# A ring of 18 panel slots, expert products in one run, a split first gather, and an earlier router in a two-block kernel

## The chip, the cores and the metric

The kernel runs on one core of one Trainium2 chip. The metric is the device time of one execution in microseconds (us); less is better.

## What is computed

The input is 512 tokens of width 1024 in fp32. A first block (token mixer, cross-attention, MLP) is followed by a second one. The part at the end of the second block is what most of the change touches:

```python
# second block, in outline
x = x + mixer(...)                        # windowed attention (8 heads) and gated linear attention, then w_out
logits = rmsnorm(x) @ w_router            # 16 experts
# every expert takes the 64 tokens of the largest affinity
# for its tokens: y = (silu(t @ w_gate) * (t @ w_up)) @ w_down, scaled by the affinity, added into x
x = x + sigmoid(rmsnorm(x) @ w_ple_gate) * (p @ w_ple)
out = rmsnorm(x)
```

Each expert has three matrices of 1024x1024 in fp32 (4 MB each). The 16 experts together read 201 MB, which is most of the 328 MB that the kernel reads.

## The kernel before

The program is written by hand for each engine: a block for TensorE (PE), ScalarE (ACT), VectorE (DVE), GpSimd (POOL) and SyncE (SP), with semaphores between them. No planner orders anything; the order in each block is the order on the engine. SP issues nearly all loads, in one queue. PSUM has 8 banks. `STAGES` (line 47) lists each use of a bank in program order; `bank_claim` waits until the last user of a bank has released it, `bank_written` until it is full, and `bank_done` until it is read out.

**Dense products** (`product_steps`, line 574, matmul at L609). Weights come in parts of 512 KB into four raw buffers (`raw`, L247; the load is L2740). POOL splits each part into a high and a low fp32r half (`split_parts_of`, L648 and L649). Each product of 128x128 by 512 is three matmuls on the halves. In `attn_pe` (L1492) and `gla_pe` such steps fill the time between dependent steps.

**Attention** (`attn_pe`, `attn_act` L1525, `attn_dve` L1566). For a pair of heads: scores (L1500), mask (DVE, L1578), maxima (L1585, L1586), powers (ACT, L1544 to L1546), shares (DVE, L1591 to L1594), turns (L1506), outputs (L1515). Between these, ACT reads the banks of the projections that fill TensorE's time (`att_evacuate`, L1480). For the first pair it reads three banks and then computes the powers of heads 0 and 1.

**Router** (PE L2188 to L2246). When the product out2 is done, its rows are turned (`norm_ffn`), a p product (`ple_product`, L1991) follows, then the router (L2211), its sum over four groups (L2217), the softmax on DVE and ACT, the turn affT (L2225), eight rounds of top-8 on DVE (L2658, L2659), and the slots. Seven further p products and `keep_busy` fillers (L501) stand between. ACT copies each p product out (L1997), stores them to HBM in `p_keep` and scales the rows (L424).

**Experts** (L1819 to L1985 and `expert_pe`, L1907). Experts go in 8 pairs; the two of a pair use the two halves of the array's columns (`x_rows`). For a pair: gather its tokens (L1895, 32 matmuls for each half of the features), DVE applies a gain (L1962), then the products gate, up and down (`expert_product`, L1850, matmul at L1864), the turn of the hidden values (L1920) and the scatter (L1882). A product reads 8 panels of 1 MB in four quarters of two panels. In each pair the order on TensorE is gate, scatter of the pair before, up, first half of the next gather, turn, second half, down. DVE adds the scattered rows to X (`add_dve`, L716) ahead of the hidden product (L1977). For pair 0 both halves of the gather stand ahead of everything.

**The ring.** The 192 panels go through 16 slots (`ring`, L1431), loaded by SP in order (`expert_load`, L1842). Slots are parts of memory that earlier stages use. So SP waits ahead of panel 0 for the last ygla bank, ahead of 6 for the last out2 bank, of 12 for the router and of 14 for the last p product. From panel 16 on it waits for the quarter that used the slot last: `x_used` counts quarters; at the fourth of each product it rises behind a `drain`. Behind the panels SP loads `p_keep` back (L2762) and the parts of w_ple_gate (L2764), for the last product.

## Time and profile before

| | before |
|---|---|
| median of 3 runs | 1996.89 us (1995.45 to 1999.15) |
| profiled execution, its own time | 1992.46 us |
| its span | 1990.7 us |
| PE busy | 1902.8 us, 96% |
| DVE, ACT, POOL busy | 781.1, 553.4, 998.0 us |
| HBM read | 328.01 MB |
| DMA in the slices of 1443 to 1940 us | 421 GB/s in nearly all |

Times in the rows are microseconds from the start of the span. The profiled execution is one execution; its own time lies 4.4 us below the median of the runs. A busy PE need not be at its peak. `PEclk` is the granted clock as a share of full speed.

### The profile page before, as it was taken

How to read it: one execution, taken by the hardware profiler on the slowest of the kernel's cores; microseconds unless marked ns; L12 is line 12 of the kernel's file. 1: busy time of each engine (PE TensorE's matmuls, PEld its weight loads, DVE VectorE, ACT ScalarE, POOL GpSimd, SP SyncE). 2: the span in 40 equal slices, each digit the busy share in tenths (PEclk: the TensorE clock that was granted, in tenths of full speed). 3: DMA queues.
4: the chain of work that ended last, by engine and by line, in shares of the span. 5: the costliest groups of instructions: out<-in, count | busy, mean ns of one | idle time of the engine just before them, and what ended most of it. 6: DMA issues, size and time to landing. Idle time of an engine off the chain costs nothing.

```text
span 1990.7 us, 23274 instructions
## 1 busy us (share of the span) xinstructions
PE 1902.8 (96%) x9434; PEld 1390.7 (70%) x9434; DVE 781.1 (39%) x1187; ACT 553.4 (28%) x1120; POOL 998.0 (50%) x568
## 2 busy tenths in 40 slices
PE   7999998999999999999989999999999999999988
PEld 6878887678788888888767768887854444434436
DVE  2455668561413301323545375554241221212124
ACT  4534438342412200211123442332230000000025
POOL 5796766657368877887555587446600000000012
PEclk9999999999999999999999999999999999999999
DMA  5321113322123223323322222212689999999982
GB/s 184 94 74 41 35 53 116 117 70 100 54 74 95 95 95 96 96 99 97 113 64 64 64 74 85 61 57 81 260 343 421 421 421 421 420 422 421 421 351 74
DMA packets 92697, 335.81 MB, mean 169 GB/s; under 512 B 7696, under 2 KB 9488, under 8 KB 67760
## 3 DMA queue, kind: packets, MB, share of 16 engines
q1 hardware_dynamic: 88864, 321.29, 43.2%
q10 hardware_dynamic: 3584, 12.52, 1.7%
q8 instruction: 75, 1.23, 0.3%
q0 software_dynamic: 144, 0.52, 0.1%
q14 instruction: 30, 0.25, 0.0%
HBM read 328.01 MB, written 6.29 MB: 168 GB/s over the span
## 4 chain that ended last, share of the span: by engine, by line
PE 78%; DMA 7%; POOL 6%; DVE 4%; ACT 3%; issue 1%; SPq 1%; PEldq 0%; ACTq 0%; DVEq 0%; PEld 0%; POOLq 0%
PE bank L609 48%; PE bank L1864 12%; DMA arena<-in_w_exp_up 3%; PE bank L1895 3%; POOL shared_r L667 2%; DMA shared<-in_w_exp_up 1%; DMA arena<-in_w_exp_gate 1%; DMA arena<-in_w_exp_down 1%; PE bank L786 1%; PE bank L630 1%; POOL shared_r L648 1%; POOL shared_r L649 1%; PE bank L1882 1%; PE bank L1068 1%; PE bank L1450 1%
## 5 line engine op out<-in xcount | busy, mean ns | idle before, releaser
L609 PE MATMUL bank<-shared_r 128*128 128x512 f32 (+1 forms) x3888 | 898.7, 387 | 18.0 <-POOL shared_r L667 7.3
L609 PEld LDWEIGHTS bank<-shared_r 128*128 128x128 f32 x3888 | 703.2, 189 | 174.4 <-issue 14.7
L648 POOL TENSOR_TENSOR shared_r<-shared,small 128x1024 fp32r<-128x1024 f32 (+1 forms) x172 | 335.3, 1949 | 847.9 <-DMA shared<-in_w_ple_gate 493.7
L649 POOL TENSOR_TENSOR shared_r<-shared,shared_r 128x1024 fp32r<-128x1024 f32 (+1 forms) x172 | 424.3, 2467 | 13.5
L1864 PE MATMUL bank<-arena 128*64 128x512 f32 x768 | 170.5, 595 | 9.8 <-DMA arena<-in_w_exp_up 3.8
L1864 PE MATMUL bank<-shared,arena 128*64 128x512 f32 x768 | 170.8, 594 | 9.4 <-DMA shared<-in_w_exp_gate 3.2
L609 PE MATMUL bank<-shared_r,arena_r 128*128 128x512 f32 x768 | 176.1, 391 | 0.0
L609 PEld LDWEIGHTS bank<-shared_r,arena_r 128*128 128x128 f32 x768 | 144.2, 188 | 31.6
L667 POOL TENSOR_TENSOR shared_r<-shared,shared_r 128x1024 fp32r<-128x1024 f32 x40 | 102.0, 2550 | 91.8 <-ACT shared_r L658 91.8
L1864 PEld LDWEIGHTS bank<-shared,arena 128*64 128x64 f32 x768 | 57.4, 137 | 116.9 <-issue 106.7
L1864 PEld LDWEIGHTS bank<-arena 128*64 128x64 f32 x768 | 56.0, 137 | 117.3 <-issue 103.3
L2344 ACT ACTIVATE arena<-arena 128x512 f32<-128x512 f32 x32 | 20.2, 633 | 219.3 <-DVE arena L2554 218.9
L609 PE MATMUL bank<-arena_r,shared_r 128*128 128x512 f32 x336 | 79.2, 396 | 0.8 <-issue 0.8
L609 PEld LDWEIGHTS bank<-arena_r,shared_r 128*128 128x128 f32 x336 | 62.9, 188 | 16.3 <-issue 1.2
L716 DVE TENSOR_TENSOR X<-bank,X 128x512 f32<-128x512 f32 x56 | 34.1, 680 | 97.0 <-PE bank L1882 97.0
L786 PE MATMUL bank<-arena 128*128 128x64 f32 x448 | 57.0, 271 | 11.7 <-DVE arena L924 6.6
L495 DVE SCALAR_TENSOR_TENSOR X<-bank,small,X 128x512 f32<-128x512 f32 x16 | 11.9, 746 | 142.4 <-PE bank L609 142.4
L786 PEld LDWEIGHTS bank<-arena 128*128 128x128 f32 x448 | 55.0, 191 | 17.2 <-issue 10.6
L2554 DVE TENSOR_SCALAR arena<-bank 128x512 f32<-128x512 f32 x32 | 21.9, 684 | 106.9 <-PE bank L609 106.5
L1895 PEld LDWEIGHTS bank<-arena 128*128 128x128 f32 x512 | 58.3, 192 | 7.8 <-issue 7.8
L1895 PE MATMUL bank<-arena 128*128 128x128 f32 x512 | 60.1, 276 | 1.9 <-issue 1.9
L1977 DVE TENSOR_TENSOR bc<-bank,bc 128x512 f32<-128x512 f32 x16 | 16.7, 1043 | 114.2 <-PE bank L1864 112.4
(428 smaller groups left out, 2072.4 us busy)
## 6 DMA issues: line engine op xcount, KB each, us to landing
shared<-in_w_in SPq DMA_DIRECT2D x80, 512.0 KB, 3.6
arena<-in_w_exp_gate SPq DMA_DIRECT2D x32, 1024.0 KB, 25.5
shared<-in_w_exp_gate SPq DMA_DIRECT2D x32, 1024.0 KB, 25.8
shared<-in_w_exp_up SPq DMA_DIRECT2D x32, 1024.0 KB, 23.4
arena<-in_w_exp_up SPq DMA_DIRECT2D x32, 1024.0 KB, 24.2
arena<-in_w_exp_down SPq DMA_DIRECT2D x32, 1024.0 KB, 25.7
shared<-in_w_exp_down SPq DMA_DIRECT2D x32, 1024.0 KB, 26.1
shared<-in_w_up SPq DMA_DIRECT2D x32, 512.0 KB, 3.6
```

Of the source, the lines that this page charges most:

```text
L609: ins = pe.matmul(dst, W_, x_, start=first, stop=final)
L630: ins = pe.matmul(bank[:, :], x[b][:, k, j * P:(j + 1) * P], halves[a][:, kk, :], start=k == 0 and (a, b) == (0, 0), stop=k == KT - 1 and ...
L648: link(pool.tensor_tensor(hi, raw(p), small[:, 18:19].to_broadcast([P, hi.shape[1]]), ALU.add))
L649: pool.tensor_tensor(lo, raw(p), hi.bitcast(F32), ALU.subtract).then_inc(S_("w_split"), 1)
L667: pool.tensor_tensor(lo, raw(p), hi.bitcast(F32), ALU.subtract).then_inc(S_("w_split"), 1)
L716: bank_release(dve.tensor_tensor(xs, bank[:, :], xs, ALU.add), n)
L786: ins = pe.matmul(bank[:, h * 64:(h + 1) * 64], HKL[g % 4][:, h, :], HQL[g % 4][:, h, :], start=True, stop=True)
L1068: ins = pe.matmul(bank[:, d * 256:d * 256 + CW], WT[:, d, s, t * P:(t + 1) * P], VM[:, s, h, :], start=(s == srcs[0]), stop=(s == srcs[-1]))
L1864: ins = pe.matmul(banks_[h][x_rows(e), :], stay, panel[:, kk, h * 512:(h + 1) * 512], start=k == 0, stop=k == KT - 1)
L1895: ins = pe.matmul(bank[:, dd * P:(dd + 1) * P], XS[:, j, d * P:(d + 1) * P], OH[:, j].rearrange("p e c -> p (e c)"), start=j == 0, stop=j ...
L2344: link(act.activation(HR[:, f % 4, :], HR[:, f % 4, :], ACT.Square))
L2554: bank_release(dve.tensor_scalar(HR[:, f % 4, :], bank[:, :], 0.0, None, ALU.max), n)
```

## The change

- The ring has 18 slots; the two new ones (`spare`) come first. SP waits for ygla ahead of panel 2, for the last split of out2 ahead of 8, for the last out2 bank ahead of 10, for the router ahead of 14 and for the last p product ahead of 16.
- The wait for a free slot is for `x_used`, which counts three quarters of each product, or for the written bank at the fourth; the `drain` is gone.
- On TensorE gate and up follow each other; the scatter of the pair before comes behind them. On DVE the additions come behind the hidden products.
- For pair 0: half 0 of the gather, two quarters of gate, half 1, the other two quarters.
- The router stands ahead of all p products; one filler instead of three stands ahead of slotT.
- In the attention the powers of head 0 stand ahead of the first evacuations.
- The load of norm_final moves from POOL to SP. The loads of w_ple_gate stand ahead of that of `p_keep`, both in other places of memory.

The diff, cut to its core (the squares of the last norm and the scratch of POOL's descriptors, which also change place or size, are left out, as are the like moves in the order of ACT's copies and DVE's reads):

```diff
-RING = 16
+RING = 18
-ARENA = 26960
+ARENA = 26768
...
+    spare_at = -(-nc.sbuf_base // 32) * 32
+    spare = sb("spare", [P, 2 * XPANEL])
+    spare_r = nc.alloc_sbuf_tensor_at("spare_r", [P, 2 * XPANEL], F32R, offset=spare_at)
...
     def raw(p):
-        return shared[:, 2 * PANEL + 1024 * (p % 4):2 * PANEL + 1024 * (p % 4) + parts[p]["kp"] * parts[p]["n"]]
+        of, at, n = shared, 2 * PANEL + 1024 * (p % 4), parts[p]["kp"] * parts[p]["n"]
+        if p >= late:
+            of, at = arena, ring_at + 6 * XPANEL + 1024 * (p % 4)
+        return of[:, at:at + n]
...
-        if p >= late + 2 and (p - late) % 6 >= 2:
-            at = ring_at + XPANEL * (4 + (p - late) % 6 - 2)
+        if p >= late and (p - late) % 6 < 2:
+            at = XPANEL * ((p - late) % 6)
+            return spare_r[:, at:at + n], spare_r[:, at + n:at + 2 * n]
+        if p >= late:
+            at = ring_at + XPANEL * ((p - late) % 6)
             return arena_r[:, at:at + n], arena_r[:, at + n:at + 2 * n]
...
+    spares = [spare[:, i * XPANEL:(i + 1) * XPANEL] for i in range(2)]
-    ring = inner[0:6] + outer[4:8] + outer[2:4] + outer[0:2] + inner[6:8]
+    ring = spares + inner[0:6] + outer[4:8] + outer[2:4] + outer[0:2] + inner[6:8]
...
         for p in range(NH // 2 + 1):
...
-            else:
-                att_evacuate(act, done, place["score", 1, 3] + 1)
             if p < NH // 2:
                 powers(2 * p)
-                if p:
-                    att_evacuate(act, done, place["out", p - 1, 0] + 1)
+                att_evacuate(act, done, place["out", p - 1, 0] + 1 if p else place["score", 1, 3] + 1)
                 powers(2 * p + 1)
...
-    x_order = [("x", 0, 0), ("x", 0, 1), ("o", 0, 0)]
+    x_order = [("x", 0, 0), ("o", 0, 0)]
     for i in range(PAIRS):
-        x_order += [("g", i, h) for h in range(2)]
+        x_order += [("g", i, h) for h in range(2)] + ([("x", 0, 1)] if i == 0 else []) + [("u", i, h) for h in range(2)]
         if i:
             x_order += [("s", i - 1, r) for r in range(8)]
-        x_order += [("u", i, h) for h in range(2)]
...
+    def panels_used(eng, q):
+        c, w, i = q // 2 % 4, q // 8 % 3, q // 24
+        if c < 3:
+            eng.wait_ge(S_("x_used"), 3 * (q // 8) + c + 1)
+        else:
+            bank_written(eng, x_bank["guy"[w], i, 1])
+
+    def slots_over(eng, slot):
+        q = slot + (2 * 4 * 3 * PAIRS - 1 - slot) // RING * RING
+        panels_used(eng, q)
...
     def expert_load(sp, q):
...
         if q >= RING:
-            sp.wait_ge(S_("x_used"), (q - RING) // 2 + 1)
+            panels_used(sp, q - RING)
...
-    def expert_product(pe, name, w, i):
-        banks_ = [bank_claim(pe, x_bank[name, i, h]) for h in range(2)]
-        for c in range(4):
+    def expert_product(pe, name, w, i, quarters=range(4)):
+        banks_ = [bank_claim(pe, x_bank[name, i, h]) if 0 in quarters else banks[BANK[x_bank[name, i, h]]] for h in range(2)]
+        for c in quarters:
...
             else:
-                ins.then_inc(bank_full[BANK[x_bank[name, i, 1]]], 1)
-                pe.drain().then_inc(S_("x_used"), 1)
+                bank_ready(ins, x_bank[name, i, 1])
...
     def expert_gather(pe, i, half):
...
-        if half == 0:
-            return
+        if half == (i > 0):
+            expert_weights(pe, i)
+
+    def expert_weights(pe, i):
         n = x_bank["o", i, 0]
...
     def expert_pe(pe, i):
-        expert_product(pe, "g", 0, i)
+        if i == 0:
+            expert_gather(pe, 0, 0)
+            expert_product(pe, "g", 0, 0, range(0, 2))
+            expert_gather(pe, 0, 1)
+            expert_product(pe, "g", 0, 0, range(2, 4))
+        else:
+            expert_product(pe, "g", 0, i)
+        expert_product(pe, "u", 1, i)
         if i:
             bank_done(pe, x_bank["o", i - 1, 0])
             expert_scatter(pe, i - 1)
-        expert_product(pe, "u", 1, i)
...
     def expert_dve(dve, i):
         expert_choice(dve, i + 1)
-        if i:
-            add_dve(dve, [x_bank["s", i - 1, r] for r in range(8)])
         for h in range(2):
...
+        if i:
+            add_dve(dve, [x_bank["s", i - 1, r] for r in range(8)])
         expert_gathered(dve, i + 1)
...
-        bank_written(pool, cell_out(H - 1, ST - 1))
-        pool.dma_start(bc[:, 0:D], A["norm_final"].partition_broadcast(P)).then_inc(S_("nf_in"), 16)
...
         router_turn(pe, out2, 1)
-        for k in range(2):
-            bank_done(pe, BASE["turn_p"] + k)
-        pe.wait_ge(S_("wp_in"), 16)
-        ple_product(pe, 0)
         pe.wait_ge(S_("wr_in"), 16)
         n = BASE["router"]
...
         bank_ready(ins, n)
+        for k in range(2):
+            bank_done(pe, BASE["turn_p"] + k)
+        pe.wait_ge(S_("wp_in"), 16)
         bank_done(pe, n)
...
-        ple_product(pe, 1)
+        ple_product(pe, 0)
         keep_busy(pe, BASE["affT"], 2, 128)
...
-        for g in range(2, 8):
+        for g in range(1, 8):
             ple_product(pe, g)
-        keep_busy(pe, BASE["slotT"], 3)
+        keep_busy(pe, BASE["slotT"], 1)
...
-        for half_ in range(2):
-            expert_gather(pe, 0, half_)
...
         for p in range(4, late):
+            if p == panels[PB["xout"]]["parts"][0]:
+                bank_written(sp, cell_out(H - 1, ST - 1))
+                sp.dma_start(bc[:, 0:D], A["norm_final"].partition_broadcast(P)).then_inc(S_("nf_in"), 16)
             load(p)
-        bank_done(sp, BASE["ygla"] + 7)
         for q in range(2 * 4 * 3 * PAIRS):
-            if q == 6:
+            if q == 2:
+                bank_done(sp, BASE["ygla"] + 7)
+            if q == 8:
+                sp.wait_ge(S_("w_split"), parts[late - 1]["split"])
+            if q == 10:
                 bank_written(sp, out2[7])
-            if q == 12:
+            if q == 14:
                 bank_done(sp, BASE["router"])
-            if q == 14:
+            if q == 16:
                 bank_written(sp, ple[7])
             expert_load(sp, q)
-        sp.wait_ge(S_("x_used"), (2 * 4 * 3 * PAIRS - RING + 2) // 2)
-        sp.dma_start(PP[:, :, :, :], p_keep.rearrange("p (i j d) -> p i j d", i=2, j=ST)).then_inc(S_("pp_in"), 16)
-        sp.wait_ge(S_("x_used"), (2 * 4 * 3 * PAIRS - RING + 10) // 2)
+        slots_over(sp, 0)
+        slots_over(sp, 16)
         for p in range(late, late + 4):
             load(p)
+        slots_over(sp, 2)
+        sp.dma_start(PP[:, :, :, :], p_keep.rearrange("p (i j d) -> p i j d", i=2, j=ST)).then_inc(S_("pp_in"), 16)
```

## Rows read from the trace of the kernel before

**Rows 1.** Windows; columns: stretch, length, busy time by engine, PEclk, DMA share, GB/s.
```profile
1600.00:1700.00 100.00, 98.45 (x525) 47.00 (x524) 23.59 (x35) 7.07 (x10) 0.00 (x0) 1.00 1.01 421
```

**Rows 2.** The chain that ended last, 1450 to 1600 us; columns: start, length, what.
```profile
1453.78 10.30 PE bank L1991 x24
...
1469.84 7.15 PE bank L1895 x64
...
1477.43 13.88 PE bank L1864 x64
...
1514.49 13.88 PE bank L1864 x64
...
1569.68 13.88 PE bank L1864 x64
```

**Rows 3.** Timeline of TensorE, the last pair; start, length, line, operation, idle before and releaser.
```profile
1888.00 3.91 PE L1882 MATMUL bank<-arena_r 128*128 128x512 f32 x16 [0.27 <-issue]
...
1905.10 3.65 PE L1864 MATMUL bank<-shared,arena 128*64 128x512 f32 x16 [1.31 <-DMA shared<-in_w_exp_up]
1910.28 1.09 PE L1920 MATMUL bank<-ident,bc 128*128 128x128 f32 x8 [1.52 <-DVE bc L1977]
...
1924.98 3.65 PE L1864 MATMUL bank<-arena 128*64 128x512 f32 x16 [1.22 <-DMA arena<-in_w_exp_down]
```

**Rows 4.** Timeline of all engines, 1395 to 1482 us: issues of SP, and POOL's last split.
```profile
1413.51 3.14 SPq L1848 DMA_DIRECT2D arena<-in_w_exp_gate  x6
...
1435.12 2.39 POOL L649 TENSOR_TENSOR shared_r<-shared,shared_r 128x1024 fp32r<-128x1024 f32 x1
...
1443.92 0.80 SPq L1848 DMA_DIRECT2D shared<-in_w_exp_gate  x2
...
1464.11 0.80 SPq L1848 DMA_DIRECT2D arena<-in_w_exp_up  x2
...
1481.05 7.67 SPq L1848 DMA_DIRECT2D arena<-in_w_exp_down  x6
```

**Rows 5.** Windows around the holes in the stream.
```profile
1432.50:1444.50 12.00, 12.00 (x59) 10.00 (x58) 2.65 (x4) 2.17 (x6) 4.29 (x2) 1.00 0.02 7
...
1464.00:1477.00 13.00, 13.00 (x95) 10.78 (x94) 4.85 (x11) 0.60 (x1) 0.00 (x0) 1.00 0.98 358
1477.00:1482.50 5.50, 5.50 (x28) 1.97 (x28) 3.17 (x5) 0.00 (x0) 0.00 (x0) 1.00 0.16 34
```

**Rows 6.** Timeline of all engines, the start of the attention.
```profile
1022.47 0.23 DVE L1586 TENSOR_SCALAR small<-small 128x4 f32<-128x4 f32 x1
...
1027.16 1.28 ACT L1544 ACT_TABLE_LOAD   x1
1027.72 4.37 PE L609 MATMUL bank<-shared_r 128*128 128x512 f32 x18
...
1030.87 0.28 ACT L1546 ACTIVATE small<-small 128x4 f32<-128x4 f32 x1
...
1031.49 2.36 POOL L649 TENSOR_TENSOR shared_r<-shared,shared_r 128x1024 fp32r<-128x1024 f32 x1
...
1031.68 3.37 DVE L1594 TENSOR_SCALAR arena<-arena,small 128x384 f32<-128x384 f32 x4
...
1037.16 2.40 PE L1506 MATMUL bank<-ident,arena 128*128 128x128 f32 x10 [5.08 <-DVE arena L1578]
...
1039.21 6.28 PE L609 MATMUL bank<-shared_r 128*128 128x512 f32 x18
```

**Rows 7.** Window behind the gap in the attention.
```profile
1038.00:1040.00 2.00, 2.00 (x10) 1.90 (x9) 0.37 (x1) 1.43 (x3) 0.00 (x0) 0.50 0.00 0
```

**Rows 8.** Timeline, DVE's half of the last norm_ffn turns.
```profile
1445.45 1.41 DVE L435 TENSOR_SCALAR shared<-bank,PT 128x512 f32<-128x512 f32 x2 [0.84 <-PE bank L445]
```

**Rows 9.** Timeline of POOL, the load of norm_final.
```profile
461.71 0.70 POOL L2062 DMA_DIRECT2D bc<-in_norm_final  x1
```

**Rows 10.** TensorE's waits: releaser, us in total, times, longest.
```profile
PE bank L1807 <- DVE arena L1795: 2.6, 1, 2.6
```

More of the change, by code:

```diff
@@ L1962, in expert_gathered, with expert_weighted @@
             bank_release(dve.tensor_tensor(XG[:, 4 * half:4 * half + 4, :], bank[:, :].rearrange("p (d c) -> p d c", d=4), gain, ALU.mult), n)
+            if half == (i > 0):
+                expert_weighted(dve, i)
+    def expert_weighted(dve, i):
         n = x_bank["o", i, 0]
@@ L2390, in _ @@
         router_act(act, out2)
-        ple_evacuate(act, 0)
         act.wait_ge(S_("rmax"), 1)
         act.activation(AFF[:, :, :], AFF[:, :, :], ACT.Exp).then_inc(S_("rexp"), 1)
-        ple_evacuate(act, 1)
+        ple_evacuate(act, 0)
         for j in range(ST):
             scale_rows(act, j)
-            ple_evacuate(act, 2 + j)
-        for g in range(2 + ST, 8):
+            ple_evacuate(act, 1 + j)
+        for g in range(1 + ST, 8):
             ple_evacuate(act, g)
@@ L2795 @@
     from concourse.bass_utils import run_bass_kernel_spmd as _run
-    nc = _bacc.Bacc("TRN2", target_bir_lowering=False, num_devices=1)
+    nc = _bacc.Bacc("TRN2", target_bir_lowering=False, num_devices=1, dynamic_dma_scratch_size=1024)
     arrays, args = {}, {}
```

2 lines of the change are left out of this document (1 added, 1 removed).

## The prediction, made before the changed kernel ran

> **What bounds the kernel now.** I read the windows of the expert stage first. From about 1482 us to 1925 us the DMA engines are full: a stretch of 100 us shows a share of 1.01 and 421 GB/s [rows 1]. The stage streams 192 panels of 1.049 MB, so one panel costs 2.49 us and a pair of panels (one quarter of a product) 4.98 us. A pair of experts has 24 panels, 59.8 us. TensorE needs less: two down products one pair of experts apart start at 1514.49 and 1569.68, 55.2 us [rows 2]. On its own it would have ended the last down product at 1514.5 + 7 x 55.2 + 13.9 - 7.8 (no gather in the last pair) = 1906.9; it ends at 1928.6, since the last quarter waits for its panels and starts at 1924.98 [rows 3]. From there to the end of the span (1990.7) 65.7 us follow, with the last scatter and the ple_gate product, and no wait for a transfer. The end is therefore the landing of the last panel plus this tail. What counts is how long the DMA engines stood idle before 1482 while panels were still to come.
>
> The timeline shows why they did. Six panels go from 1413.51, the next only at 1443.92 when the last out2 bank is written, the last two of the 16 slots at 1464.11 behind the last p product, and the seventeenth panel at 1481.05, when the first quarter has freed a slot [rows 4]. The windows show the holes: 7 GB/s from 1432.5 to 1444.5, and 34 GB/s from 1477 to 1482.5 [rows 5].
>
> Second, the attention. TensorE has a gap of 5.1 us from 1032.1 to 1037.16. The timeline leads through VectorE to ScalarE, which started the powers of head 0 only at 1027.16, behind three evacuations, though their input was there at 1022.70 [rows 6]. Behind the gap the granted clock is 0.50, the lower level (1.2 GHz) [rows 7].
>
> **The ring, and the order of loads.** Ahead of the wait for out2 stand panels 0 to 7 now, and 8 and 9 wait only for the last split of out2, which POOL ends at 1437.5 [rows 4]. Six panels were through at 1432.5; two more (5.0 us) last to 1437.5, and 8 and 9 fill 1439 to 1444. Panels 10 to 13 go at 1443.9, 14 and 15 behind the router; all are through at about 1459.5. Then the engines idle until 16 and 17 come, which wait for the last p product. So most of the first hole moves to 1460; but by the time of the first quarter 18 panels are in instead of 16. This is worth 2 x 2.49 = 5.0 us, no more, since the ring was full before and is full now.
>
> **Router ahead of p product 0.** The router claims the bank that the eighth norm_ffn turn leaves, and VectorE ends that at 1446.86 [rows 8]. It took 1.92 us from 1447.28; from 1446.95 it ends at 1448.87: 0.3 us sooner, not the 1.9 us of the p product ahead of it. Everything to the gather comes 0.3 us sooner. Seven p products now follow affT instead of six, 1.72 us each (10.30 us for six) [rows 2]: the last ends at 1465.5 instead of 1464.1. Picks come at 1466.1, so one filler is enough and nothing idles. Panels 16 and 17 go at 1465.5 instead of 1464.1; with the 2 MB that ScalarE stores they took 12.9 us to about 1477 [rows 5], so now to 1478.5 or 1479.
>
> **Gather split.** Both halves of the gather (7.15 us) stood ahead of the gate product, which began at 1477.43 [rows 2]. Now half 0 runs from 1469.5 to 1473.1; VectorE's 0.7 us for its gain, hidden before, lie open; the product starts at 1473.85. The first quarter (3.5 us) frees its slots at 1477.45, 3.6 us sooner; the second at 1480.9; half 1 and another 0.7 us follow; the third ends at 1488.7, the fourth at 1492.1. The stream: panels 18 and 19 from 1478.9, 20 and 21 to 1488.9, 22 issued at 1488.7 and moving at 1490.1, a hole of 1.2 us. Before, panel 16 began to move at 1482.55, so that at 1490.1 the stream stood at 19.05. Now it stands at 22, ahead by 2.95 panels: **7.3 us**, ring and split together. TensorE is 1 us later at the end of that gate product; of its 22 us of slack that costs nothing.
>
> **Products in one run, scatter behind them.** Drains that go (0.3 us each) give nothing while panels are the limit. Two points had to be worked out. (a) The last pair: the last up quarter can start 19.9 us before the last panel lands. It takes 3.65, the scatter 3.9, turn and evacuation 1.5, three down quarters 10.7 [rows 3]: 19.8 us. TensorE arrives as the last panel does: 0 us, with no margin, where the scatter's 3.9 us were margin before. (b) VectorE has eight additions of 0.7 us behind the hidden products; TensorE claims the banks in that order and slower. 0 us. norm_final moves from POOL's queue, where its issue took 0.70 us [rows 9], to SP's: POOL waits for TensorE behind it, and SP loads four parts ahead of use. 0 us; without that cover 0.7 us either way. The ple_gate and p_keep loads stand behind the last panel in SP's queue, and the tail didn't wait for them: 0 us.
>
> **First powers ahead of banks.** ScalarE starts at 1022.75. From table load to the sums of head 0 took 4.0 us (1027.16 to 1031.15), so VectorE gets head 0 at 1026.75. Three evacuations (1.8 us) and head 1 (2.6 us) follow: 1031.15. TensorE claims the first evacuated bank at 1029.2, and it is free at 1027.4: no new wait. Now VectorE's shares of head 1 stand where those of head 0 stood. Its four multiplications took 3.37 us there, with POOL's L649 active from 1031.49 to 1033.85; undisturbed they take 1.41 [rows 6]. I take it that head 1 meets the same: VectorE is through at 1035.05 instead of 1036.78, and TensorE goes on at 1035.45 instead of 1037.16: **1.7 us**, leaving a gap of 3.4 us. Undisturbed it would be 3.7 us; nothing and 3.7 are the bounds. The Trainium skill, SBUF — State Buffer, section "SBUF: two separate sides", says that VectorE and GpSimd lock a pair of ports for a whole instruction, and that whichever starts first gets it. By that rule VectorE may as well win here, and the sum would be 2.0 us more.
>
> The clock: 18 matmuls of the same product took 6.28 us behind the gap and 4.37 us ahead of it; of the ten transposes' 2.40 us half is the clock's: 3.1 us [rows 6, 7]. The next longest gap inside the kernel is one of 2.6 us, and the clock stayed up behind it [rows 10]. 3.4 us lie between; nearer to 2.6, so I take it that it stays up: **3.0 us**. From 1037 on TensorE has no gap up to 1151, and what POOL splits behind that is released by TensorE, so both gains reach the end.
>
> **Sum** against the profiled execution: 7.3 + 1.7 + 3.0 = 12.0 us, span 1990.7 to 1978.7, its time 1992.5 to 1980.5. The median of the three runs is 4.4 us above the profiled time: 1996.9 - 12.0 = **1984.9**. A measurement tells about 0.2% (4 us) from no change.
>
> **Rivals.**
> 1. The clock still falls behind the gap of 3.4 us. Gain 9.0, **1987.9**. For it: a gap of 5.1 us does it. Against: 2.6 doesn't. 0.24.
> 2. VectorE gets ahead of POOL: gap 1.4 us, gain 14.0, **1982.9**. Against it: POOL was ahead by 0.2 us. 0.10.
> 3. The last pair is late, or the hole at 1489 wider: at the last down quarter each microsecond is one at the end. Late by 2 us, with a hole of 4.2 us: gain 7, **1990**. 0.12.
> 4. The ring brings no lead, because 16 and 17 are not in before the first quarter asks for more. Then 2.3 us of the 7.3 and little of the attention are left: gain 3, **1994**. 0.05.
> 5. Slower: the stretch between up and down products, in which no slot comes free, grows by the scatter from 8.7 to 12.6 us in pairs 1 to 6, and the queue runs dry in each. It decides when less than some 16 us of loads (3.3 pairs of panels) are in flight at the end of the up product. By the rates above 4.6 are in flight in pair 1, and more later, so I don't expect it. If it were so: 3.9 us in each of six pairs, 23 us, less 12: **2008**. 0.04.
>
> The forecast keeps 0.45. **Range** 1979.5 to 1993: forecast and rivals 1 to 3, with the bounds of each and 2 us for the medians. Faster 0.91 (all but rivals 4 and 5), same 0.05, slower 0.04.
>
> **What would show it.** Windows: a hole near 1460 to 1466, hardly one between 1477 and 1489, 421 GB/s from there to the last panel (all less what the attention gains). Last down quarter at about 1913. TensorE's wait at L1506 3.4 us, and a granted clock of 1.00 behind it. I am wrong if the last quarter isn't released by a transfer, if GB/s falls between up and down products in the middle pairs, or if the clock shows 0.50 behind the gap.

## The result, and the profile after

The changed kernel's median is 1988.25 us over 5 executions (1985.09 to 1992.09), beside 1995.45 us (1992.79 to 1999.15, 5 executions) for the kernel before on the same chip. The ratio is 0.9961, with a 95% interval of 0.9948 to 0.9974: about 7.8 us less, between 5.2 and 10.4 (the two medians differ by 7.2). The forecast was a gain of 12.0 us and a time of 1984.9, with a range of 1979.5 to 1993.0.

| | before | after |
|---|---|---|
| profiled execution, its own time | 1992.46 us | 1989.56 us |
| its span | 1990.7 us | 1987.8 us |
| its mean granted clock | 0.996 | 0.991 |
| PE, DVE, ACT, POOL busy | 1902.8, 781.1, 553.4, 998.0 | 1905.6, 782.7, 553.5, 997.0 us |
| HBM read | 328.01 MB | 328.01 MB |

The two spans differ by 2.9 us only, since the two executions had different luck with the clock ahead of the changed places (experiment 4). So I compare stretches that begin at an event of the same work: in the attention from the scores of heads 2 and 3, first half, to their second half; in the expert stage from the issue of the first panel (1413.51 before, 1416.68 after).

**The attention.** Timeline of all engines of the changed kernel, 1018 to 1048 us (L618 is L609 of before, L1516 is L1506, L1601 is L1594, L1554 and L1556 are L1544 and L1546):

```profile
1018.25 1.28 ACT L1554 ACT_TABLE_LOAD   x1
...
1027.34 0.62 ACT L1554 ACTIVATE arena<-arena,small 128x384 f32<-128x384 f32 x1 [7.80 <-DVE small L1593]
...
1029.76 0.28 ACT L1556 ACTIVATE small<-small 128x4 f32<-128x4 f32 x1
...
1031.05 1.35 PE L1510 MATMUL bank<-arena 64*128 64x256 f32 x8
...
1031.82 1.41 DVE L1601 TENSOR_SCALAR arena<-arena,small 128x384 f32<-128x384 f32 x4
...
1034.41 1.89 POOL L657 TENSOR_TENSOR shared_r<-shared,small 128x1024 fp32r<-128x1024 f32 x1 [2.86 <-PE bank L618]
...
1034.78 4.83 DVE L1601 TENSOR_SCALAR arena<-arena,small 128x384 f32<-128x384 f32 x4
1036.39 2.35 POOL L658 TENSOR_TENSOR shared_r<-shared,shared_r 128x1024 fp32r<-128x1024 f32 x1
...
1039.99 2.22 PE L1516 MATMUL bank<-ident,arena 128*128 128x128 f32 x10 [3.29 <-DVE arena L1585]
...
1041.86 5.18 PE L618 MATMUL bank<-shared_r 128*128 128x512 f32 x18
...
1046.97 1.35 PE L1510 MATMUL bank<-arena 64*128 64x384 f32 x8
```

ScalarE now starts with the powers of head 0, and VectorE's shares of head 0 take 1.41 us instead of 3.37 [rows 6]. ScalarE's table load stands at 1018.25 now, in time in which ScalarE has nothing else to do; before, it stood at 1027.16 and delayed head 0 [rows 6]. The shares of head 1 take 4.83 us, with both steps of POOL's split beside them. TensorE's gap is 3.29 us instead of 5.08. Behind it the same ten transposes and 18 matmuls take 2.22 and 5.18 us (2.40 and 6.28 before; 4.37 for 18 at the full clock [rows 6]): the clock still falls. From scores to scores it is 15.92 us instead of 18.98.

**The start of the stream.** Timeline of SP, 1395 to 1500 us (L1867 is L1848 of before):

```profile
1416.68 0.94 SPq L1867 DMA_DIRECT2D spare<-in_w_exp_gate  x2
1417.67 3.69 SPq L1867 DMA_DIRECT2D arena<-in_w_exp_gate  x6
1440.70 12.93 SPq L1867 DMA_DIRECT2D shared<-in_w_exp_up  x8
1468.84 0.80 SPq L1867 DMA_DIRECT2D arena<-in_w_exp_down  x2
1481.10 1.01 SPq L1867 DMA_DIRECT2D spare<-in_w_exp_down  x2
1484.53 9.84 SPq L1867 DMA_DIRECT2D arena<-in_w_exp_down  x4
1496.18 0.89 SPq L1867 DMA_DIRECT2D arena<-in_w_exp_gate  x2
```

Timeline of TensorE, 1465 to 1500 us (gather L1913, expert products L1883):

```profile
1472.69 3.74 PE L1913 MATMUL bank<-arena 128*128 128x128 f32 x32
...
1477.41 3.65 PE L1883 MATMUL bank<-spare,arena 128*64 128x512 f32 x16 [0.55 <-DVE arena L1988]
1480.87 3.63 PE L1883 MATMUL bank<-arena 128*64 128x512 f32 x16
1484.43 3.84 PE L1913 MATMUL bank<-arena 128*128 128x128 f32 x32
1489.05 7.09 PE L1883 MATMUL bank<-arena 128*64 128x512 f32 x32 [0.78 <-DVE arena L1988]
```

Windows (stretch, length, busy time by engine, PEclk, DMA share, GB/s) in the same profile:

```profile
1464.00:1470.00 6.00, 6.00 (x19) 2.58 (x17) 5.20 (x12) 4.17 (x7) 0.00 (x0) 1.00 0.12 27
1480.00:1484.00 4.00, 4.00 (x22) 1.54 (x18) 0.00 (x0) 0.00 (x0) 0.00 (x0) 1.00 0.81 283
1481.50:1482.00 0.50, 0.50 (x4) 0.17 (x2) 0.00 (x0) 0.00 (x0) 0.00 (x0) 1.00 0.11 41
1484.00:1492.00 8.00, 7.22 (x50) 4.71 (x48) 1.98 (x3) 0.00 (x0) 0.00 (x0) 1.00 1.01 428
1492.00:1500.00 8.00, 8.00 (x40) 2.73 (x38) 0.00 (x0) 3.42 (x3) 0.00 (x0) 1.00 0.82 286
1493.00:1493.50 0.50, 0.50 (x6) 0.21 (x4) 0.00 (x0) 0.00 (x0) 0.00 (x0) 1.00 0.00 0
1540.00:1640.00 100.00, 100.00 (x536) 48.04 (x534) 22.20 (x33) 8.69 (x12) 0.00 (x0) 1.00 1.01 421
```

The hole is at 1464 to 1470, as forecast. Behind it the stream is nearly whole, but not quite: at a mean of 283 and 286 instead of 421 GB/s it loses 1.3 us from 1480 to 1484 and 2.6 us from 1492 to 1500. These are short stops and not a slower stream throughout: within them it stands at 41 GB/s from 1481.5 to 1482 and at 0 from 1493 to 1493.5, just behind the issue of the next pair of panels. From 1500 to 1900 it runs at 421 or 422 GB/s.

**The end of the stream.** Timeline of TensorE, 1895 to 1930 us (scatter L1900, turn L1946):

```profile
1901.72 3.65 PE L1883 MATMUL bank<-arena 128*64 128x512 f32 x16 [1.31 <-DMA arena<-in_w_exp_up]
1905.31 3.92 PE L1900 MATMUL bank<-arena_r 128*128 128x512 f32 x16
1909.07 1.03 PE L1946 MATMUL bank<-ident,bc 128*128 128x128 f32 x8
1910.56 7.09 PE L1883 MATMUL bank<-arena 128*64 128x512 f32 x32 [0.45 <-ACT arena L1961]
1917.45 3.63 PE L1883 MATMUL bank<-shared,arena 128*64 128x512 f32 x16
1922.05 3.65 PE L1883 MATMUL bank<-shared,arena 128*64 128x512 f32 x16 [0.97 <-DMA shared<-in_w_exp_down]
```

The last down quarter still waits for its panels. It starts 505.37 us behind the first panel's issue, where it was 1924.98 - 1413.51 = 511.47. The tail behind it is 65.75 us, as before (65.7).

### The profile page after: what moved, and what is told of

Same layout as the page of the kernel before. It is cut to its first block, busy times and chain, and to the rows that moved or that the text cites. A ratio compares the mean times of both kernels' runs of the same rounds, so it can differ in the third digit from the quotient of the medians.

```text
span 1987.8 us, 23241 instructions
## 1 busy us (share of the span) xinstructions
PE 1905.6 (96%) x9430; PEld 1395.6 (70%) x9430; DVE 782.7 (39%) x1187; ACT 553.5 (28%) x1120; POOL 997.0 (50%) x567
## 3 DMA queue, kind: packets, MB, share of 16 engines
HBM read 328.01 MB, written 6.29 MB: 168 GB/s over the span
## 4 chain that ended last, share of the span: by engine, by line
PE 78%; DMA 7%; POOL 7%; DVE 4%; ACT 3%; issue 1%; SPq 0%; ACTq 0%; DVEq 0%; POOLq 0%
PE bank L618 48%; PE bank L1883 11%; PE bank L1913 3%; DMA arena<-in_w_exp_up 3%; DMA shared<-in_w_exp_up 3%; POOL shared_r L676 2%; PE bank L1900 1%; DMA shared<-in_w_exp_down 1%; PE bank L795 1%; POOL shared_r L658 1%; PE bank L639 1%; POOL shared_r L657 1%; PE bank L1077 1%; PE bank L1460 1%; PE bank L2022 1%
## 5 line engine op out<-in xcount | busy, mean ns | idle before, releaser
L618 PE MATMUL bank<-shared_r 128*128 128x512 f32 (+1 forms) x3840 | 891.1, 388 | 15.0 <-POOL shared_r L676 6.7
L618 PEld LDWEIGHTS bank<-shared_r 128*128 128x128 f32 x3840 | 697.9, 190 | 169.4 <-issue 14.7
L658 POOL TENSOR_TENSOR shared_r<-shared,shared_r 128x1024 fp32r<-128x1024 f32 (+1 forms) x170 | 419.5, 2468 | 13.4
L657 POOL TENSOR_TENSOR spare_r<-arena,small 128x1024 fp32r<-128x1024 f32 x2 | 3.8, 1895 | 482.8 <-DMA arena<-in_w_ple_gate 482.8
L618 PE MATMUL bank<-shared_r,arena_r 128*128 128x512 f32 x768 | 176.1, 391 | 0.0
L618 PEld LDWEIGHTS bank<-shared_r,arena_r 128*128 128x128 f32 x768 | 144.2, 188 | 31.5
L1883 PE MATMUL bank<-arena 128*64 128x512 f32 x688 | 154.6, 599 | 11.0 <-DMA arena<-in_w_exp_up 9.8
L1883 PE MATMUL bank<-shared,arena 128*64 128x512 f32 x672 | 147.7, 593 | 8.6 <-DMA shared<-in_w_exp_up 7.7
L676 POOL TENSOR_TENSOR shared_r<-shared,shared_r 128x1024 fp32r<-128x1024 f32 x38 | 96.8, 2547 | 96.0 <-ACT shared_r L667 96.0
L1883 PEld LDWEIGHTS bank<-arena 128*64 128x64 f32 x688 | 49.6, 138 | 108.9 <-issue 93.5
L1883 PEld LDWEIGHTS bank<-shared,arena 128*64 128x64 f32 x672 | 48.3, 137 | 105.1 <-issue 93.9
L2370 ACT ACTIVATE arena<-arena 128x512 f32<-128x512 f32 x32 | 20.3, 633 | 219.2 <-DVE arena L2579 218.7
L618 PE MATMUL bank<-arena_r,shared_r 128*128 128x512 f32 x336 | 79.5, 396 | 0.8 <-issue 0.8
L618 PEld LDWEIGHTS bank<-arena_r,shared_r 128*128 128x128 f32 x336 | 63.1, 188 | 16.4 <-issue 1.2
L1913 PEld LDWEIGHTS bank<-arena 128*128 128x128 f32 x512 | 58.9, 192 | 2.1 <-issue 1.6
L1913 PE MATMUL bank<-arena 128*128 128x128 f32 x512 | 60.0, 275 | 0.0
```

What stands on the lines that cost most here:

```text
L618: ins = pe.matmul(dst, W_, x_, start=first, stop=final)
L657: link(pool.tensor_tensor(hi, raw(p), small[:, 18:19].to_broadcast([P, hi.shape[1]]), ALU.add))
L658: pool.tensor_tensor(lo, raw(p), hi.bitcast(F32), ALU.subtract).then_inc(S_("w_split"), 1)
L676: pool.tensor_tensor(lo, raw(p), hi.bitcast(F32), ALU.subtract).then_inc(S_("w_split"), 1)
L1883: ins = pe.matmul(banks_[h][x_rows(e), :], stay, panel[:, kk, h * 512:(h + 1) * 512], start=k == 0, stop=k == KT - 1)
L1913: ins = pe.matmul(bank[:, dd * P:(dd + 1) * P], XS[:, j, d * P:(d + 1) * P], OH[:, j].rearrange("p e c -> p (e c)"), start=j == 0, stop=j ...
```

## The experiments

"Stream to up" and "stream to down" are the times from the first panel's issue to the last up and the last down quarter; "attention" is the stretch from scores to scores; all from the one profile of each kernel. The time is the median of all executions, the ratio is to the kernel before on the same chip.

| kernel | time us | ratio (95%) | attention | stream to up | stream to down |
|---|---|---|---|---|---|
| before | 1995.45 | 1 | 18.98 | 491.59 | 511.47 |
| after | 1988.25 | 0.9961 (0.9948 to 0.9974) | 15.92 | 485.04 | 505.37 |
| e1_attention_only | 1995.65 | 0.9988 (0.9979 to 0.9997) | 15.96 | 491.87 | 511.75 |
| e2_all_but_attention | 1990.94 | 0.9971 (0.9959 to 0.9982) | 18.90 | 485.09 | 505.10 |
| e3_gather_not_split | 1989.93 | 0.9961 (0.9948 to 0.9975) | 15.94 | 486.33 | 507.3 |
| e4_ring_of_16 | 1992.63 | 0.9980 (0.9971 to 0.9989) | 15.93 | 490.17 | 510.40 |
| e5_fill_two_gaps | 1987.05 | 0.9952 (0.9939 to 0.9965) | 14.31 | 485.85 | 505.73 |
| e6_scatter_between | 1987.97 | 0.9956 (0.9943 to 0.9968) | 15.90 | 484.90 | 504.92 |
| e7_router_behind_p | 1989.6 | 0.9960 (0.9946 to 0.9974) | 15.92 | 485.12 | 505.03 |
| e8_before_filled | 1993.95 | 0.9988 (0.9979 to 0.9997) | 16.10 | 491.52 | 511.40 |
| e9_fill_five_gaps | 1985.81 | 0.9941 (0.9928 to 0.9955) | 14.32 | 483.93 | 503.88 |
| e9_again | 1985.06 | 0.9940 (0.9929 to 0.9952) | 14.31 | 484.30 | 504.26 |
| e10_fill_the_right_gaps | 1989.55 | 0.9961 (0.9947 to 0.9974) | 14.31 | 484.05 | 505.10 |

The kernel before had medians of 1997.44 (beside e1 to e4), 1996.88 (e5, e6, e8, e9) and 1997.64 (e7, e9_again, e10).

### 1. The attention alone, and all the rest

e1 is the kernel before with the new order of the powers; e2 is the changed kernel with the old order:

```diff
-            else:
-                att_evacuate(act, done, place["score", 1, 3] + 1)
             if p < NH // 2:
                 powers(2 * p)
-                if p:
-                    att_evacuate(act, done, place["out", p - 1, 0] + 1)
+                att_evacuate(act, done, place["out", p - 1, 0] + 1 if p else place["score", 1, 3] + 1)
```

Expected of e1: 

> The kernel before with the attention edit alone (powers of head 0 ahead of the three evacuations). Theory A (mine): TensorE's gap at the first turns shrinks from 5.1 to about 3.3 us, 1.8 us gained for good; the clock still falls there for about half as long, 3.4 instead of 6.8 us, so 1.3 us more in the mean: 3.1 us below the kernel before at the same clock elsewhere. The expert stage is as before: holes of 12 us and 5.5 us in the stream. Theory B (the lower mean clock in the changed kernel comes from the attention edit): the granted clock over the run is lower than that of the kernel before by 0.003 or more here too, and the gain is 0 or less.

Expected of e2: 

> The changed kernel with the attention as before. Theory A: TensorE's gap is 5.1 us again, with a low clock of 6.8 us behind it; the expert stage keeps its lead of 6.1 us from the first expert load to the last panel, so the time is 6 us below the kernel before, 3 us above the changed kernel at the same clock elsewhere. Theory B (the new places in memory or the moved load of norm_final lower the clock in the first 1000 us): the clock over the run is lower than that of the kernel before in all runs, and the start of the attention is reached 3 us or more later than in the kernel before.

Measured: 0.9988 and 0.9971, that is 2.4 and 5.8 us of 1997, each to about 2 us, together 8.2 where the whole change has 7.8. So the two halves add up within these intervals, and nothing shows that one eats the other's gain. By stretches e1 gains 3.0 us in the attention and nothing in the stream, e2 0.1 and 6.4 us. The gap in e1 is 3.34 us, with a granted clock behind it as in the changed kernel. Theory A holds for both; theory B of e1 does not (its mean clock over the executions is 0.9928, that of the kernel before 0.9919).

### 2. The parts of the lead

e3 has both halves of the first gather ahead of the gate product, e4 the ring of 16 slots with SP's waits at the panels two lower, e7 the router behind p product 0 (and with it the order of ACT's copies and the three fillers of before); cut to the core:

```diff
e3:
             expert_gather(pe, 0, 0)
-            expert_product(pe, "g", 0, 0, range(0, 2))
             expert_gather(pe, 0, 1)
-            expert_product(pe, "g", 0, 0, range(2, 4))
+            expert_product(pe, "g", 0, 0)
...
e4:
-RING = 18
+RING = 16
...
-    ring = spares + inner[0:6] + outer[4:8] + outer[2:4] + outer[0:2] + inner[6:8]
+    ring = inner[0:6] + outer[4:8] + outer[2:4] + outer[0:2] + inner[6:8]
...
e7:
+        for k in range(2):
+            bank_done(pe, BASE["turn_p"] + k)
+        pe.wait_ge(S_("wp_in"), 16)
+        ple_product(pe, 0)
         pe.wait_ge(S_("wr_in"), 16)
         n = BASE["router"]
...
```

Expected of e3: 

> The changed kernel with both halves of the first gather ahead of the gate product. Theory A: the first quarter ends 3 us later, and the DMA engines stand idle until then, but the small holes of 1480 to 1500 (3.7 us of transfer lost there in the changed kernel) close: lead over the kernel before 4.5 to 5 us instead of 6.1, so the split is worth 1 to 1.5 us, not the 2 us of the forecast. Rival: the small holes are of the ring's order of loads and stay; then the lead falls to 3 us or less, and the split is worth 3 us.

Expected of e4: 

> The changed kernel with 16 slots (without the two new ones), all other parts of the change in place. Theory A: two panels less are in before the first quarter, so the last panel lands 5.0 us later than in the changed kernel, counted from the first expert load: lead over the kernel before 1 us. Rival (the lead comes from the earlier first quarter, and the ring's two slots only fill a hole that would be filled anyway): the lead stays above 3 us.

Expected of e7: 

> The changed kernel with the router behind p product 0, as before. Theory (the router's move brings 0.3 us to the first gather, since the norm_ffn turns set its start): the router's first matmul 1.9 us later behind the last turn's end than in the changed kernel less what it waited there (1.33 us idle), so the first gather 0.2 to 0.6 us later, the last up quarter 0.2 to 0.6 us later behind the first expert load; time 1988 to 1990, not to be told from 1988.3. Rival (the move is worth its whole p product): the gather and the last up quarter 1.9 us later, 1990 to 1991.

The lead is how much sooner behind the first panel's issue a quarter starts than in the kernels with the old order. Three kernels have the old ring, gather and router (before, e1, e8), eight have all that is new (after, e2, e5, e6, e7 but for the router, e9 twice, e10). At the last up quarter the former stand at 491.52 to 491.87, mean 491.66, the latter at 483.93 to 485.85, mean 484.79: 6.9 us of lead. At the last down quarter it is 511.54 less 504.92: **6.6 us**, with single profiles up to about 1 us to either side. e4 lacks 5.4 us of the lead at the last up quarter, so the two slots bring 5.4; e3 lacks 1.5, so the split brings 1.5, each with that same scatter. The rival of e4 is refuted.

Of e3 theory A is right, in its size and in its reason. Windows of e3, and of the changed kernel for the second stretch:

```profile
1480.00:1484.00 4.00, 4.00 (x20) 1.29 (x18) 0.57 (x1) 0.00 (x0) 0.00 (x0) 1.00 0.25 51
1484.00:1500.00 16.00, 16.00 (x78) 5.35 (x76) 0.00 (x0) 3.42 (x3) 0.00 (x0) 1.00 1.01 422
```

```profile
1484.00:1500.00 16.00, 15.22 (x88) 7.44 (x86) 1.98 (x3) 3.42 (x3) 0.00 (x0) 1.00 0.92 357
```

Without the split there is one long hole, until the first quarter has freed its slots, and none behind it. It is so in all four kernels without the split: in 16 us that begin 5 us behind the issue that the first quarter released, before, e1, e3 and e8 have 424 or 425 GB/s, and the nine with the split 351 to 379. e4 is among the nine, with 353, so it isn't the ring. The split frees the first slots sooner and gives part of that back: in the changed kernel SP issues no panel from 1484.90 to 1492.75, while TensorE does half 1 of the gather and the third quarter, and the stream stops at 1493.

In the times e4 shows its loss, just clear of the intervals (0.9980 beside 0.9961); e3 does not.

e7 is the router's move by itself. Its first gather comes 1473.64 - 1417.43 = 56.21 us behind the first panel's issue, 56.01 in the changed kernel: 0.2 us, not 1.9. The last up quarter is the same to 0.1 us.

e3's last pair shows how thin the cover there is. Timeline of its TensorE, 1895 to 1930 us:

```profile
1901.06 5.35 PE L1883 MATMUL bank<-arena 128*64 128x512 f32 x16 [2.36 <-DMA arena<-in_w_exp_up]
1906.34 3.92 PE L1900 MATMUL bank<-arena_r 128*128 128x512 f32 x16
...
1918.53 7.06 PE L1883 MATMUL bank<-shared,arena 128*64 128x512 f32 x32
```

Here TensorE waited 2.36 us for an up panel, the granted clock fell (0.63 in the window 1902.6 to 1906), and the quarter took 5.35 us instead of 3.65. The last two down quarters then run on without a wait: the end was set by TensorE, 0.9 us behind where the panels would have set it (507.3, against 504.9 of the others and the 1.5 us that this kernel is behind them). In the other profiles the last quarter waits for its panels.

### 3. The scatter's place

e6 has the scatter, and VectorE's additions, between gate and up again, without the drains and with the ring of 18 (cut to TensorE's part):

```diff
-        expert_product(pe, "u", 1, i)
         if i:
             bank_done(pe, x_bank["o", i - 1, 0])
             expert_scatter(pe, i - 1)
+        expert_product(pe, "u", 1, i)
```

Expected: 

> The changed kernel with the scatter between gate and up products again (and VectorE's additions ahead of the hidden products). Theory A: the last panel lands at the same time, TensorE waits some 4 to 5 us for it instead of 1.0, lead unchanged (6 to 6.5 us over the kernel before), time the same as the changed kernel's within 0.5 us, since panels are the limit. Rival 5 of the forecast (the long stretch without a free slot empties the queue): then this kernel would be faster, by 2 us or more, with less idle time of the DMA engines between 1540 and 1800.

Timeline of e6's TensorE, 1895 to 1930 us:

```profile
1902.09 3.65 PE L1884 MATMUL bank<-arena 128*64 128x512 f32 x16 [1.31 <-DMA arena<-in_w_exp_up]
1907.27 1.09 PE L1947 MATMUL bank<-ident,bc 128*128 128x128 f32 x8 [1.53 <-DVE bc L2009]
...
1917.11 3.65 PE L1884 MATMUL bank<-shared,arena 128*64 128x512 f32 x16 [1.20 <-DMA shared<-in_w_exp_down]
1922.11 3.65 PE L1884 MATMUL bank<-shared,arena 128*64 128x512 f32 x16 [1.35 <-DMA shared<-in_w_exp_down]
```

Time and stream are those of the changed kernel (1987.97 and 1988.25; 504.92 and 505.37). TensorE has more idle time here, since the scatter's 3.9 us no longer stand in the last pair behind the up product, and it is of no use: the panels set the end either way. The product order behind the scatter costs nothing and brings nothing.

### 4. The clock behind the gap

A filler is a matmul whose result nobody reads. e8 is the kernel before with five fillers ahead of the first turn of the attention, e5 the changed kernel with three, and with two ahead of the turn of the gated linear attention. The lines are e5's; e8 has the first two alone, with 5 in place of 3:

```diff
             nn = att_bank[what, h, x]
+            if (what, h, x) == ("turn", 0, 0):
+                keep_busy(pe, BASE["proj_g"] + 6, 3)
             bank = bank_claim(pe, nn)
...
     def gla_turn(pe, half):
+        if half == 0:
+            keep_busy(pe, BASE["turn_gla"], 2)
         pe.wait_ge(S_("gla_o"), half + 1)
```

Expected of e8: 

> The kernel before with five filler matmuls (4.3 us) in its 5.1 us gap of the attention, nothing else. Theory C: the gap's own 5.1 us stay, the low clock of 6.8 us behind it goes: scores of heads 2 and 3 to their second half 15.9 us instead of 19.0, 3.1 us below the kernel before. Rival (the fall of the clock costs less than the 3.1 us that I charged to it, because VectorE sets the pace behind the gap): under 1.5 us.

Expected of e5: 

> The changed kernel with filler matmuls in two gaps of TensorE: three (2.6 us) in the 3.3 us ahead of the attention's first turns, two (1.7 us) in the 2.6 us ahead of the first turns of the linear attention. Theory C (now mine: the clock falls behind any gap of about 1.8 us or more in some executions, and always behind 3.3 us): no low clock behind either place; scores of heads 2 and 3 to their second half 14.7 us instead of 15.9, and 1.6 us less up to the first expert load. Some 2 to 3 us below the changed kernel, 10 to 11 below the kernel before. Rival (fillers count for nothing, since the clock looks at something else or falls at fixed times): the clock still falls there and the time is that of the changed kernel.

Timeline of TensorE in e8, 1028 to 1048 us (fillers L501, turn L1508, product L609):

```profile
1033.99 4.45 PE L501 MATMUL bank<-ones,ident 128*128 128x512 f32 x10
1039.23 1.31 PE L1508 MATMUL bank<-ident,arena 128*128 128x128 f32 x10 [0.79 <-DVE arena L1580]
1040.30 4.37 PE L609 MATMUL bank<-shared_r 128*128 128x512 f32 x18
```

In e8 VectorE is as late as before, but the turn takes 1.31 us instead of 2.40, and the 18 matmuls 4.37 instead of 6.28: 3.0 us. That is what the low clock behind the gap cost before; the prediction worked out 3.1 and entered 3.0 in its sum. The stretch gains 18.98 - 16.10 = 2.9 us. In e5 the same two groups take 1.31 and 4.35 us, and the stretch is 14.31, another 1.6 us below the changed kernel's. The times agree but are too coarse to decide: e8 is 2.4 us (0.6 to 4.2) below the kernel before, e5 9.6 us, where the changed kernel has 7.8, with intervals that overlap.

In the changed kernel 1.3 us of the 3.0 were gained: the granted clock is low for 3.4 us behind the gap instead of 6.8. It is so in all six profiles whose gap is about 3.3 us (after, e1, e3, e4, e6, e7); with the old order of powers (before and e2, gaps of 5.08 and 5.36 us) it is 6.8, and in the five profiles with fillers there is no low stretch.

The other half of e5 did nothing. Its fillers stand ahead of the first half of the gated linear attention's turn; the gap is ahead of the second half. That gap also shows why the prediction was too sure of the clock. Timeline of TensorE around it, in the kernel before and in the changed one (the first of the two lines of each is the turn, L1807 and L1814):

```profile
1359.27 1.97 PE L1807 MATMUL bank<-ident,arena 128*128 128x128 f32 x16 [2.61 <-DVE arena L1795]
1360.99 5.38 PE L609 MATMUL bank<-arena_r,shared_r 128*128 128x512 f32 x22
```

```profile
1360.82 3.47 PE L1814 MATMUL bank<-ident,arena 128*128 128x128 f32 x16 [2.62 <-DVE arena L1802]
1363.94 2.36 PE L618 MATMUL bank<-arena_r,shared_r 128*128 128x512 f32 x8
```

The gap is the same to 0.01 us. In the one execution of before that the prediction rested on, the clock stayed up behind it and the 16 transposes took 1.97 us; in the changed kernel they take 3.47. All eleven other profiles in which the gap is open show a low clock behind it. The same is seen in the first block, at gaps of 1.8 to 2.5 us at about 16, 140, 175, 255 and 356 us, and behind two of 0.87 and 0.67 us at 324 to 326: the profile of before has one low stretch there, e4 two, the changed kernel five, e6 six, with the same gaps. e1 has five with before's layout of memory and before's load of norm_final, so neither of these is needed for it. The profile of before was one of its luckier executions: its mean clock is 0.996, the mean over 22 executions of that kernel 0.9919. This is why the scores of heads 2 and 3 start at anything from 1026.4 to 1031.8 us in the profiles without e10's, and why the spans of two profiles say little about a change of 10 us.

### 5. A version that beats both

e9 is e5 with two fillers more at each of three levels of the first block's mixer; it was run in two sets, the second as e9_again. e10 is e9 with fillers moved to where the gaps are:

```diff
e9, against e5:
                 g = m * NL + x
+                if (m, x) in ((0, 0), (0, 5), (2, 5)):
+                    keep_busy(pe, n, 2)
                 pe.wait_ge(S_("h_q"), g + 1)
e10, against e9:
-                if (m, x) in ((0, 0), (0, 5), (2, 5)):
-                    keep_busy(pe, n, 2)
+                if (m, x) in ((0, 0), (0, 5), (5, 5)):
+                    keep_busy(pe, n, 4 if m else 2)
...
+        keep_busy(pe, BASE["norm_mem"], 4)
         pe.wait_ge(S_("mem_xs"), 1)
...
-        if half == 0:
-            keep_busy(pe, BASE["turn_gla"], 2)
+        if half == 1:
+            keep_busy(pe, BASE["turn_gla"] + 4, 5)
```

Expected of e9: 

> As the one with two gaps filled, and two fillers each in the three gaps of 2.2 to 2.5 us in the first mixer (levels 0 and 5 of chunk 0, level 5 of chunk 2). Theory C: the mean clock over the runs rises from 0.992 to 0.995 or more, each 0.001 worth 1.2 to 1.7 us, so about 4 to 5 us below the changed kernel and 12 below the kernel before; the runs scatter less. Rival (the low clocks in the first mixer are no result of the gaps): the low stretches near 142 and 255 us stay, and this kernel is as fast as the one with two gaps filled.

Expected of e9_again: 

> The kernel with five gaps filled, once more, beside the one with the fillers moved. Its fillers ahead of the first half of the gated linear attention's turn and of level 5 of chunk 2 stand at places without a gap. Theory (filling the gap in the attention and one or two in the first block is worth 2 us against the changed kernel): 1985 to 1987, and low stretches behind the gaps at about 254, 322 and 1360 again. Rival (the first measurement was luck of the chip): 1987 to 1989, as the changed kernel.

Expected of e10: 

> The kernel with five gaps filled, with two of the five fillers moved to the gaps that they had missed, and one more gap filled. In its profile the gaps before 252.95 (2.45 us), 321.42 (2.28 us) and 1357.92 (2.61 us) stand unfilled, and the granted clock is low behind each, for 3.4, 6.8 and 3.4 us. Now four fillers of some 0.45 us stand ahead of level 5 of chunk 5, four ahead of the turn of the memory's rows, and five ahead of the second half of the gated linear attention's turn. Theory (a fall of the clock costs about half of its low stretch, and whoever fills a gap of 1.8 us or more avoids it): none of the three low stretches is left; at half of 13.6 us this would be 6.8 us, but by what single falls have cost here (1.25 us for each 3.4 us) it is 4 x 1.25 = 5.0 us; so 1981 to 1984 where the other has 1985.8. Rival (the fall is not set by these gaps: it comes at another place of the same stage): the low stretches stay within some us of the same places, and the time is the same, 1984 to 1988.

e9 has 1985.81 and 1985.06 us, ratios 0.9941 and 0.9940: 4 us below the changed kernel and 12 below the kernel before by the ratios, as expected of e9, on two sets, and with the least scatter (1983.66 to 1986.38 over 11 executions). Two of its five filler places stand where there is no gap. The gaps of 2.2 us at 140 are filled in both profiles, and the clock stays up there, as theory C had it. Of the low stretches that were expected of e9_again at about 254, 322 and 1360 the first did not come, with its gap of 2.45 us open; the other two did.

e10 is 4.5 us slower than e9 beside it, though its profile has the highest mean clock of all (0.997) and two low stretches instead of three. Timeline of its TensorE in the three places:

```profile
252.81 5.37 PE L510 MATMUL bank<-ones,ident 128*128 128x512 f32 x8 [2.54 <-DVE arena L944]
258.02 1.00 PE L797 MATMUL bank<-arena 128*128 128x64 f32 x8
...
323.21 3.70 PE L510 MATMUL bank<-ones,ident 128*128 128x512 f32 x8 [0.67 <-ACT arena L1113]
...
1358.31 4.46 PE L510 MATMUL bank<-ones,ident 128*128 128x512 f32 x10
1362.60 1.91 PE L1821 MATMUL bank<-ident,arena 128*128 128x128 f32 x16
```

Two mistakes of mine can be read here. A filler is two records, so four of them take 3.70 us, not the 1.8 that I had reckoned; five take 4.46 in a gap of 2.61. And at 252.81 the fillers come behind the gap: they claim the bank of that level, and the claim waits for the same VectorE work as the level itself. 5.37 us are added there and none saved. At the two other places the next turn starts 4.2 us behind the product ahead of it where e9 has 2.3, and 4.3 where it has 2.6. So the expectation failed by its fillers' cost and place. Of its two theories the first is right on one point: behind the turn at 1362.60 the clock is up (1.91 us for 16 transposes). Whether the same fillers, fewer and on a free bank, would bring the rest was not tried.

## Why the forecast was right in kind and 3.4 us too low

**The ring and the split (forecast 7.3, found 6.6).** Panels set the end, before and after; the tail is unchanged. The two slots bring 5.4 (forecast 5.0). The split and the router bring 1.5 of a forecast 2.3. The size that failed is "a hole of 1.2 us": around it SP issues one pair of panels per quarter, the stream runs at 283 and 286 GB/s in two windows, and loses 3.9 us by the rate of 421: two stops, where the forecast had one. The stop at 1493 and what is lost behind it come with the split (experiment 2). By the landing of the 32nd panel, just behind these windows, the changed kernel leads by 5.1 us, and the eight kernels with all that is new by 4.8 to 6.6, mean 5.8; at the last panel it is 6.1, and 6.5 in the mean. So the lead is 1.5 us short of the forecast there and 0.7 at the end. Why it grows in between I can't account for; single profiles scatter by as much.

**Router.** Forecast 0.3, found 0.2 in e7.

**The last pair, scatter behind up.** "TensorE arrives as the last panel does", 0 us, no margin. From the last up quarter TensorE would have been there after 20.33 - 0.97 = 19.4 us (forecast 19.8), the panel comes after 20.3 (forecast 19.9). The cost is 0 as forecast. Rival 3, a late last pair or a wider hole, is half true: the hole was wider, the pair was not late; that it can be is seen in e3's profile.

**The attention itself (forecast 1.7, found 1.8).** Gap 5.08 to 3.29. POOL held VectorE as assumed, and longer: 4.83 us instead of 3.37 for four such operations. But ScalarE was through with head 1 sooner than reckoned, since the forecast had left the table load of 1.28 us on the path, and VectorE could start 3.73 us behind the scores of heads 2 and 3 (1034.78 - 1031.05), where the forecast had 5.24. It was through after 8.56 us; the forecast had 8.61. Two misses of 1.5 us cancel: that the size came out is luck. The rule that GpSimd and a VectorE operation in a mode with two ports lock the shared pair of ports for a whole instruction (the Trainium skill, SBUF — State Buffer, section "SBUF: two separate sides") fits with this row, though no row shows the mode. POOL started 0.37 us ahead. The first of VectorE's four operations took 1.75 us and ended at 1036.52, 0.2 us behind POOL's first step; the second took 2.50 us and ended at 1038.94, 0.2 us behind its second; the last two took 0.41 us each, as undisturbed ones do. Rival 2, VectorE ahead of POOL, is refuted.

**The clock (forecast 3.0, found 1.3).** This is the step that failed, with the larger part of the difference: "3.4 us lie between; nearer to 2.6, so I take it that it stays up". The price was right (e8: 3.0 us for the whole fall); the condition was wrong. It rested on one gap in one execution, and the eleven other profiles with that gap show the contrary. Rival 1 had the event, the clock still falls, but not its price: the low stretch is half as long. Its 1987.9 is 0.35 us from the result, a little better than it deserves.

**The sum.** By stretches 3.1 + 6.6 = 9.7 us against 12.0. The times say 7.8, 5.2 to 10.4. (From 1996.9, the median that the forecast started from, it is 8.6; the five executions of before beside the changed kernel had 1995.45.) The remaining 1.9 us between profiles and times lie inside that interval, and no run settles them. The mean granted clock of the timed executions may hint at one cause, though the difference is smaller than the third decimal to which each clock is given: 0.9919 over 22 executions of before, 0.9922 over 5 of after, where half of a low stretch of 3.4 us less should give 0.0009 more.

**Rival 4** (no lead from the ring) is refuted by e4, whose lead is 5.4 us shorter, **rival 5** (the queue runs dry between up and down products) by 421 GB/s in all windows from 1540 to 1900 us and by e6. **norm_final and the order of the last loads**: 0 us; the tail is the same to 0.1 us. Norm_final alone was not tried.

**The signs.** The hole came at 1464 to 1470 and the last down quarter was released by a transfer, as named. It started at 1922.05 and not at 1913: 2.8 us through the attention and the stream, and 6.2 us through the part ahead of the attention and the gap at 1360, where the profile of before had met the clock better. The wait at L1506 was 3.3 us (named 3.4), and the clock behind it showed 0.50 for a while, which the prediction had named as the sign against it.

## What to carry over

In a stage that streams without a pause, count the panels that are in before the consumer asks for more: each slot more is worth one panel's transfer time once, if it can be filled before the consumer frees one, here 2 x 2.49 us forecast and 5.4 found, and the work that TensorE must do after the last panel is the other half of the sum. A statement on the clock needs more than one execution: take the profiles of unrelated kernels of the same program, and look at the same gap in each. A filler must claim a bank whose last reader is done before the gap begins, and its length must be read from a row before it is counted.

## What was not expected of the hardware

- TensorE's granted clock fell to the lower level behind gaps of 1.8 to 2.6 us, and behind a pair of under 1 us, in some executions and not in others, with the same gaps: at about 1360 us behind 2.61 us in eleven profiles of twelve. In the changed kernel and e2 it also fell at 1712 and 1715 us, at gaps of 2.2 and 2.3 us between expert products, where the panels are the limit. The low stretch at the gap of 2.2 us near 140 us lasted 3.4 us in some profiles, 6.8 in e5 and e6, and 10.2 in e7. A gap of 3.3 us was followed by a low stretch of 3.4 us in six of six, gaps of 5.1 and 5.4 us by 6.8 us in two of two. Filling the gap in the attention took the low stretch away in five of five, and was worth 1.6 us in the changed kernel and 2.9 us in the kernel before.
- VectorE lost 3.4 us, not 2.0, to POOL when both steps of a split fell beside it (4.83 us for 1.41 us of work): one operation of VectorE was held until each step ended.
- Around the first gate product, where SP had issued no more than a pair of panels in the microseconds before, the mean was 283 to 286 GB/s over 4 and 8 us, with the stream at 0 from 1493 to 1493.5; SP had issued the next pair at 1492.75, 0.7 us ahead of the last landing. With a full ring it ran at 421.
